# Two layers of a hybrid-attention decoder on one core: where head group C's halves stand, and how its pages are loaded

## The reference, cut to what matters

```python
oa = dilated_attend(qa, ka_all, va_all, wbuf + jnp.arange(t), rel_bias)          # A: 6 heads, window cache
ob = dsa_attend(qb, qi, wi, q_pos, ki_all, gather_kv, ..., rel_bias)             # B: 6 heads, top-k keys, paged
kc_all = jnp.concatenate([paged_rows(cache_c_k), kc], axis=1)                    # C: 4 heads x 64 values, paged
vc_all = jnp.concatenate([paged_rows(cache_c_v), vc], axis=1)
oc = diff_attend(qc, kc_all, vc_all, q_pos, lam_l, lam_init, subln_g_l, rel_bias)
o = jnp.concatenate([oa.reshape(nb, t, -1), ob.reshape(nb, t, -1), oc.reshape(nb, t, -1)], axis=-1)
```

## Time and profile before

| | us |
|---|---|
| median of 3 runs | 1349.34 |
| lowest, highest | 1344.23, 1352.64 |
| the profiled execution | 1351.34 |
| its span | 1349.6 |

### The profile page before, as it was taken

The page is one execution under the profiler, slowest core; times in us unless marked ns, Lnnn a source line. Parts: engine busy times, 40 slices in busy tenths (PEclk is TensorE's granted clock), DMA queues, the critical chain, the costliest instruction groups (busy, mean ns, idle before and its releaser), DMA issues.

```text
span 1349.6 us, 23207 instructions
## 1 busy us (share of the span) xinstructions
PE 1281.5 (95%) x8038; PEld 803.8 (60%) x8038; DVE 495.5 (37%) x1433; ACT 265.4 (20%) x683; POOL 59.9 (4%) x265
## 2 busy tenths in 40 slices
PE   6898899989999999999999999998899999999998
PEld 3544356645657666666666445664556577767775
DVE  1103568865672111011040165876766511101113
ACT  0121144322123111000022112542221411100001
POOL 1000011100001000000010000110100100000000
PEclk9999999998999999999999999998999999999999
DMA  9899899999874687868754688999996456776663
GB/s 376 246 318 280 280 328 360 342 349 350 268 247 151 210 302 251 328 237 322 277 212 158 224 284 285 337 345 351 352 343 224 152 192 210 245 270 217 210 215 138
DMA packets 190814, 363.83 MB, mean 270 GB/s; under 512 B 23072, under 2 KB 141608, under 8 KB 189034
## 3 DMA queue, kind: packets, MB, share of 16 engines
q1 hardware_dynamic: 156192, 345.62, 74.5%
q10 hardware_dynamic: 34506, 16.74, 4.6%
HBM read 354.20 MB, written 58.40 MB: 306 GB/s over the span
## 4 chain that ended last, share of the span: by engine, by line
PE 71%; SPq 15%; DMA 5%; issue 4%; DVE 4%; DVEq 1%; ACT 1%; ACTq 0%
PE psf L1148 23%; PE psf L1623 21%; SPq L556 11%; PE psf L1526 4%; DMA ring<-in_tiles 3%; PE psf L1607 3%; PE psf L1169 2%; PE psf L1350 2%; PE psf L1397 2%; PE psf L1465 2%; PE psf L1232 1%; SPq L566 1%; SPq L548 1%; PE psf L1521 1%; PE psf L1430 1%
## 5 line engine op out<-in xcount | busy, mean ns | idle before, releaser
L1148 PE MATMUL psf<-hT,ring 128*128 128x320 f32 x1184 | 326.3, 435 | 5.5 <-DMA ring<-in_tiles 5.1
L1148 PEld LDWEIGHTS psf<-hT,ring 128*128 128x128 f32 x1184 | 224.1, 191 | 109.7 <-issue 16.7
L1623 PE MATMUL psf<-big,ring 128*128 128x320 f32 x1024 | 278.0, 433 | 2.1 <-DVE big L2113 2.1
L1623 PEld LDWEIGHTS psf<-big,ring 128*128 128x128 f32 x1024 | 193.7, 190 | 86.8 <-issue 3.4
L2113 DVE TENSOR_TENSOR big<-sq 128x320 f32<-128x320 f32 x64 | 31.5, 493 | 239.1 <-ACT sq L1117 238.8
L1723 DVE TENSOR_SCALAR rstd<-psf,adaT 128x256 f32<-128x256 f32 x40 | 19.3, 482 | 235.8 <-PE psf L1623 231.9
L1350 PE MATMUL psf<-big,qs 128*32 128x512 f32 x512 | 69.3, 637 | 9.9 <-DMA big<-in_pool_bk 9.6
L1117 ACT ACTIVATE sq<-psf 128x320 f32<-128x320 f32 x64 | 28.0, 438 | 231.8 <-PE psf L1148 220.9
L1074 ACT ACTIVATE sq<-xT 128x320 f32<-128x320 f32 x32 | 15.1, 471 | 289.9 <-DVE xT L1736 276.7
L1397 PE MATMUL psf<-big,ptbuf 128*32 128x128 f32 x2048 | 64.0, 278 | 4.2 <-DMA big<-in_pool_cv 4.2
L1397 PEld LDWEIGHTS psf<-big,ptbuf 128*32 128x32 f32 x2048 | 55.5, 111 | 10.8 <-issue 9.0
(11 more groups left out here) (219 smaller groups left out, 1351.5 us busy)
## 6 DMA issues: line engine op xcount, KB each, us to landing
ring<-in_tiles SPq DMA_DIRECT2D x246, 512.0 KB, 4.4
big<-in_cache_a SPq DMA_DIRECT2D x64, 768.0 KB, 7.1
out_cache_a<-in_cache_a SPq DMA_DIRECT2D x64, 768.0 KB, 5.4
big<-in_pool_bk SPq DMA_DIRECT2D x128, 192.0 KB, 6.0
big<-in_pool_bv SPq DMA_DIRECT2D x128, 192.0 KB, 6.6
big<-in_pool_cv SPq DMA_DIRECT2D x192, 64.0 KB, 5.3
big<-in_tiles SPq DMA_DIRECT2D x22, 512.0 KB, 7.7
big<-in_pool_ck SPq DMA_DIRECT2D x128, 64.0 KB, 4.1
```

The costliest lines, as they stand in the source:

```text
L1148: ins = pe.matmul(ps[:, 0:T], ring[:, s, k, :], rhs[:, k, :], start=k == 0, stop=k == KD - 1)
L1623: ins = pe.matmul(bank[6 + m % 2][:, 0:T], ring[:, s, k, :], uT[:, KD * q + k, :], start=q + k == 0, stop=q == 3 and k == KD - 1)
```

## The change

Units 0 to 3 now take C's first half of sequences 0 to 3 and units 4 to 7 the second half of the same sequences. Units 8 and up take both halves of sequences 4 to 7 in pairs: 8 and 9 sequence 4, 10 and 11 sequence 5, 12 and 13 sequence 6, 14 and 15 sequence 7. A's and B's sequences are as before. For the last three sequences ACT loads C's pages whole, in rows of 1024 bytes, into one of two stores, for two units at once; SP loads none of C's values for them. Since a unit's half of C no longer goes with A or B, `sbias[0]` and `sbias[1]` now go with C's half; A's rows in them are overwritten by B's (`load_rows`) in each layer and restored before the next. The four `parts` are issued one by one, each one turn ahead of its use.

```diff
-        self.q, self.k, self.qc, self.kc = (QB, KB, QC + 1, KC + 1) if self.second else (QA, KA, QC, KC)
+        self.c, self.half = (n % 4, n // 4) if n < NB else (n // 2, n % 2)
+        self.whole, self.store = n >= NB + 2, n // 2 % 2
+        self.q, self.k, self.v, self.o = (QB, KB, VB, 4) if self.second else (QA, KA, VA, 0)
+        self.qc, self.kc, self.vc, self.oc = QC + self.half, KC + self.half, VC + P * self.half, 3 + 4 * self.half
...
+            def load_rows(e, second):
+
+                for g in range(3):
+                    sp.dma_start(sbias[e][G * g:G * g + 2 * NT, :],
+                                 bass.AP(dist_s.tensor, (HA * second + 2 * g) * row + NT - 1,
+                                         [[row, 2], [H * NDIST - 1, NT], [1, L]])).then_inc(ld_rows[e], 16)
...
-                    if u.n == len(LATE) - 1:
+                    if u.n + 1 in PARTS:
 
                         sp.wait_ge(tile_used, used(MID[l][-1]))
-                        for m in PARTS.values():
-                            sp.dma_start(parts[m].rearrange("p k m -> p (k m)"),
-                                         a["tiles"][l * TILES + WO_AT + m, :, 0:3 * P]).then_inc(ld_parts, 16)
+                        m = PARTS[u.n + 1]
+                        sp.dma_start(parts[m].rearrange("p k m -> p (k m)"),
+                                     a["tiles"][l * TILES + WO_AT + m, :, 0:3 * P]).then_inc(ld_parts[m], 16)
...
+                    if u.n == 4:
+
+                        sp.wait_ge(u_logit.sem, u_logit.done(l, 3))
+                        load_rows(0, True)
+                    if u.n == 7:
+
+                        sp.wait_ge(u_logit.sem, u_logit.done(l, 7))
+                        load_rows(1, True)
...
-                    load_c(l, then, was, 1, range(NPG // 2 if then.second else NPG))
+                    if then.second and not then.whole:
+                        load_c(l, then, pages(then.c, CHECKED), 1, range(NPG // 2))
+                    elif not then.second:
+                        load_c(l, then, was, 1)
...
+                        if l + 1 < DEPTH and d in (10, 12):
+                            load_rows(d // 2 - 5, False)
...
+                def load_whole(pool, places, signal, at):
+
+                    for j in range(NPG):
+                        act.dma_start(places[j // (NPG // 2)][:, j % (NPG // 2), :],
+                                      pool[ds(at[j] + l * N_PHYS, 1)].rearrange("o p w -> (o p) w")).then_inc(signal, 16)
...
+                    then = UNIT[u.n + 3] if u.n in (7, 9, 11) else None
+                    if then:
+
+                        at = pages(then.c, CHECKED)
+                        if u.n == 7:
+                            act.wait_ge(tile_used, used(MID[l][-1]))
+                        act.wait_ge(u_s.sem, u_s.done(l, u.n))
+                        load_whole(a["pool_ck"], whole_k[then.store], ld_wk[then.store], at)
+                    then = UNIT[u.n + 2] if u.n in (8, 10, 12) else None
+                    if then:
...
+                        act.wait_ge(u_o.sem, u_o.done(l, u.n - 1))
+                        load_whole(a["pool_cv"], whole_v[then.store], ld_wv[then.store], at)
...
+                    if u.c != u.b:
+                        zc = TS - NT - NT * u.c
+                        pe.transpose(bank[2][0:TS, 352:384], znew[3 * G:P, zc:zc + TS], ident[3 * G:P, 3 * G:P])
...
+                    if u.n in (NB, NB + 1):
+
+                        dve.wait_ge(ld_rows[u.half], 48 * (2 * l + 1))
...
-                        ins = dve.tensor_copy(oT[q, u.o:u.o + 4, t0:t0 + NT],
-                                              bass.AP(first.tensor, first.offset, [list(first.ap[0]), [2 * NT, 4], [1, NT]]))
+                        part = bass.AP(first.tensor, first.offset, [list(first.ap[0]), [2 * NT, 3], [1, NT]])
+                        dve.tensor_copy(oT[q, u.o:u.o + 3, t0:t0 + NT], part)
+                        ins = dve.tensor_copy(oT[q, u.oc, tc:tc + NT], bank[3][q, P + NT * (6 + half):P + NT * (7 + half)])
```

More of the change, by code:

```diff
@@ L277, in program @@
                  for i, m in enumerate(PARTS.values())}
+        flat = lambda x: x[:, :, :].rearrange("p k t -> p (k t)")
+        four = KD * P
+        whole_k = [[fours(kv[:, s, CK_AT:CK_AT + four]) for s in range(2)],
+                   [fours(flat(hT)[:, 3 * P * len(PARTS):3 * P * len(PARTS) + four]), fours(flat(zT[:, QI:QI + 4, :])[:, 0:four])]]
+        whole_v = [[fours(kv[:, s, CV_AT:CV_AT + four]) for s in range(2)],
+                   [fours(workbuf[:, 0:four]), fours(wkibuf[:, 0:four])]]
         ik = [x[:, 0:PAST].rearrange("p (j w) -> p j w", j=NPG)
@@ L346, in program @@
         ld_more = [sem(f"ld_more{j}") for j in range(2)]
-        ld_parts = sem("ld_parts")
+        ld_parts = {m: sem(f"ld_parts{m}") for m in PARTS.values()}
         ld_late = {i: sem(f"ld_late{i}") for i in HOMED}
@@ L354, in program @@
         ld_dist = sem("ld_dist")
+        ld_wk = [sem(f"ld_wk{s}") for s in range(2)]
+        ld_wv = [sem(f"ld_wv{s}") for s in range(2)]
+        ld_rows = [sem(f"ld_rows{e}") for e in range(2)]
         st_dist = sem("st_dist")
@@ L573, in load_c @@
             def load_c(l, u, at, half, which=range(NPG)):
-                load_pages(l, at, a["pool_cv" if half else "pool_ck"], P * u.second, (ck_in, cv_in)[half][u.s],
+                load_pages(l, at, a["pool_cv" if half else "pool_ck"], P * u.half, (ck_in, cv_in)[half][u.s],
                            (ld_ck, ld_cv)[half][u.s], which)
@@ L670, in load_keys, with pages_of @@
                         load_c(l, u, at, 0)
-                at = pages(2, CHECKED)
+                def pages_of(u):
+                    return pages(u.b if u.second else u.c, CHECKED)
+                at = pages_of(UNIT[2])
                 sp.wait_ge(u_s.sem, u_s.done(l, 0))
@@ L810, in _ @@
                 for u in UNIT:
-                    pool.wait_ge(z_set.sem, z_set.done(l, MADE_AT[QB + 2 if u.second else QC]))
+                    pool.wait_ge(z_set.sem, z_set.done(l, MADE_AT[QB + 2 if u.second else u.qc]))
                     pool.wait_ge(u_s.sem, u_s.free(l, u.n))
-                    t0 = TP + NT * u.b
+                    t0, tc = TP + NT * u.b, TP + NT * u.c
                     for half in range(2):
@@ L1047, in _ @@
                         exp_item(slots[0])
-                    was = at
-                    if NB <= u.n + 3 < UNITS:
-                        at = pages(UNIT[u.n + 3].b, CHECKED)
+                    if u.n + 3 in (NB, NB + 1):
+                        at = pages(UNIT[u.n + 3].c, CHECKED) if u.n + 3 == NB else at
                         load_c_keys(UNIT[u.n + 3], at)
@@ L1906, in read_logits @@
                     dve.wait_ge(u_tp.sem, u_tp.free(l, u.n))
+                    if u.n in (NB, NB + 1):
+                        dve.wait_ge(ld_rows[u.half], 48 * (2 * l + 1))
+                    elif l and u.n in (0, 4):
+                        dve.wait_ge(ld_rows[u.half], 48 * 2 * l)
                     dve.sem_inc(passed, 1)
-                    dve.tensor_tensor_reduce(out=S[:, 0, :], in0=psf[:, 0:L], in1=sbias[u.second][:], scale=1.0,
+                    dve.tensor_tensor_reduce(out=S[:, 0, :], in0=psf[:, 0:L], in1=sbias[u.half][:], scale=1.0,
                                              scalar=-3e38, op0=ALU.add, op1=ALU.max, accum_out=mx[:, u.s, 0:1])
```

57 lines of the change are left out of this document (35 added, 22 removed).

## The result

The changed kernel took **1368.35 us** (median of 4 runs, 1358.74 to 1369.74), the kernel before 1348.24 in runs beside it; the ratio is **1.0145**, 95% interval 1.0118 to 1.0171. The forecast was 1361 us within 1340 to 1372: the range holds it, the side is right (slower), the sum was 8 us too small. By the bound of one per cent it is slower, which had the chance 0.27. The profiled execution took 1367.81 us, its span is 1366.0 against 1349.6.

What follows compares the result with a forecast made beforehand. PE carries 71% of the chain, but in the sample attention data, not arithmetic, decide. Unit 10's wait +4.6 and +3.7 us, unit 11's values +1.4, PE and DVE +2.0: +11.7 on 1349.3 gives 1361 us, range 1340 to 1372.

Steps and rivals of the forecast that it cites:

- two engines: Bias-row DMAs in SP's turns 4 and 7: source's outer dimension 2, so two engines carry 24 rows each, 4.1 us.
- PE and DVE: Units of both layers: one more transpose in 11 units a layer and two more copies per unit, together +2.0 us.
- The price of a set: Three DMAs of 16 bias rows, twice in a layer's units: each set costs 3.7 us of wall where queues overlap.
- The first set ... about 4 us of slack, so no stall there: Bias rows issued in turn 4: unit 6's values, tightest behind them, still land in time, with about 4 us of slack.
- The new wait of DVE: Unit 9's logits, layer 0: DVE must have the second set of bias rows, so it stands 4 to 5 us.
- The later of the two, not their sum: Around units 9 and 10: DVE's wait for bias rows and PE's for unit 10's keys overlap; only the later counts.
- waits for unit 10's `pool_bk` at about 8.5 and 9 us: Sign that the forecast is right: PE's waits for unit 10's B keys grow from 3.91 and 5.49 us to these.
- The packet price: DMA engine time: 11.2 ns fixed per packet plus 38.3 us per MB, so 512 bytes cost 30.8 ns, 1024 bytes 50.4.
- "faster" rival: Bias rows cheap and all six pairs of whole rows a layer pay back, -8.8 us in both layers: 1340 us; chance 0.18.
- Parts: Output-weight parts leave the queue ahead of unit 10's keys: -2.1 us at that wait, +1.05 at unit 11's values, layer 0.
- Theory A: Follow-up runs' theory: the cost is that a 16-row bias DMA with outer source dimension 2 runs on two engines.

## Why the prediction was right and where it was wrong

The range and the side were right, and two engines were the main cause as forecast. But the sum came near by luck in part: a stall that the sum held at nothing cost 8 us, and other terms erred the other way. By place, profiled executions, in us:

| | forecast | measured |
|---|---|---|
| layer 0, first logits to `turn_far` of unit 7 | 0 | +8.0 |
| layer 0, on to unit 10 | +4.6 | +4.4 |
| layer 0, on to the output projection | +1.4 | -2.9 |
| layer 1, up to unit 8 | 0 | +0.5 |
| layer 1, on to unit 10 | +3.7 | +3.4 |
| layer 1, on to the output projection | 0 | +1.3 |
| PE and DVE, wherever | +2.0 | in the rows above |
| dense stretches | 0 | +1.8 |
| sum | +11.7 | +16.4 |

**Two engines: right, and shown.** Widening the DMAs takes 1.05 points out of the change's 1.45, with the same bytes and the same time of issue. Narrow ones cost 1.41% added to the kernel before, wide ones 0.60%. And the packets show bias rows two at a time in the one case and up to eight in the other.

**The price of a set: near, for the first one.** 3.7 us were forecast; 0.97 MB are missing behind it in layer 0, 2.8 us, and its own bytes (0.2 MB, 0.6 us) come on top. Part of that is SP's issue, in which the engines ran dry. In layer 1 only 0.28 MB are missing in the 20 us around the first set. The two engines were held longer than the 4.1 us of the forecast: 48 rows took 9.4 to 11.3 us of engine time in all, so 4.7 to 5.6 on each of two, spread over 5.3 to 8.3.

**"The first set ... about 4 us of slack, so no stall there": wrong, in layer 0.** This is the step that failed. PE waited 4.95 us and lost another 1.7 by the lower clock. The slack was spent twice. I had priced SP's issue of three DMAs at 1.3 us and called it covered by data under way; it took 2.12 us, and the cover ran out while it lasted, since the engines emptied meanwhile (7 and 3 tenths ahead of the dip). Unit 6's values were issued 3.3 us later; the slowest landed 8.1 us after its issue, not 5.6; and PE wanted them at 253.75, 1.6 us earlier than before, as its first logits had begun 2.0 us earlier. Against that the slack of the page that lands last was not 4 us but 2.3 (247.4 + 5.6 = 253.0, wanted at 255.32; I had reckoned with a page of median landing): 3.3 + 2.5 + 1.6 - 2.3 = 5.1 us, against 4.95 measured. In layer 1 the wait for unit 6's values is 0.84 us, where the kernel before had 1.53, so the step held there. With 8-row DMAs SP issues as long; layer 0 then has no wait for these values, layer 1 one of 3.06 us.

**The new wait of DVE: right in kind, its size in neither layer.** Forecast 4 to 5 us; measured 3.02 and 8.14. In layer 0 the stall at unit 6 had moved PE and with it DVE's need of the rows.

**"The later of the two, not their sum": right in layer 1, in part in layer 0.** In layer 1 PE's old wait for unit 10's keys, 5.49 us, became 0.19, and 6.62 us stand before it on DVE's account. In layer 0 the 2.15 us on DVE's account are followed by 2.60 for C's whole keys, which ACT issues last. So "waits for unit 10's `pool_bk` at about 8.5 and 9 us", which I had named as the mark, was wrong: the same loss has another name and place in the profile, and its sum by place (+4.4 and +3.4 us) came out as forecast.

**The packet price: right.** The changed kernel's DMA from 308 to 345 us:

```profile
DMA packets 10971, 13.58 MB, mean 367 GB/s; under 512 B 1220, under 2 KB 10965, under 8 KB 10965
...
q1 hardware_dynamic: 7718, 10.54, 82.0%
q10 hardware_dynamic: 3247, 2.95, 24.2%
q8 instruction: 4, 0.07, 0.8%
```

107.0% of 16 x 37 us are 633 us; 10971 x 11.2 ns and 13.58 x 38.3 us give 643. (A share above 1.0 needs no second queue: q1 alone stood at 104.8%.) But it bought nothing. The forecast counted +2.2 - 0.7 for whole rows at units 10 to 12 in layer 0 and +1.1 in layer 1; measured without the exchange they cost 0.5%, some 7 us, and from unit 12 on alone as much, where I had counted nothing. Why is open. The "faster" rival (packets decide) falls.

**Parts: right in the mechanism, nothing in the sum.** At unit 10's wait in layer 0 -2.1 us were forecast, -2.7 measured with the parts alone, and 4.1 us of new waits followed (1.40 and 2.68), where I had expected 1.05.

**PE and DVE, +2.0: too much.** With all of it in and neither exchange nor whole rows the ratio is 0.9982. The new transposes and the split copies of the outputs are short, as priced (duration ns, min/median/max), and `turn_near` waits for the copies 1.9 us in three places, before 2.3 in two:

```profile
L1446 PEld LDWEIGHTS psf<-ident,znew x22: 103/105/125, 226.7 to 1018.9; 32*64 32x64 f32 x22
...
L2044 DVE COPY oT<-psf x44: 166/180/186, 247.6 to 1041.5; 64x24 f32<-64x24 f32 x44
...
L2045 DVE COPY oT<-psf x44: 146/155/163, 247.7 to 1041.6; 64x8 f32<-64x8 f32 x44
```

**What stays open.** Theory A accounts for 15 of the 20 us between the medians (1368.35 - 1353.08). The rest, about 5 us, is some of whole rows and some of the exchange's bytes, and doesn't add up: exchange (8 rows a DMA) alone +0.6%, whole rows alone +0.5%, both +0.4%, and the exchange with halves +0.9%. The first of these had the four parts ahead of the second set and the others had not, so their differences are not those of the named edits alone; no run adds the exchange to the parts alone. Single executions of the changed kernel lie up to 11 us apart (1358.74 to 1369.74), so the waits of one profiled execution can't settle a few tenths of a per cent.

## What to carry to other kernels

Count the engines of a DMA before its bytes: four sets of 0.2 MB cost 1.4% in three DMAs each, and 0.6% in six each. A wait that goes at one unit in a stretch where data decide is a wait at the next: three edits here (the second set earlier, whole keys earlier, the parts) moved one by 2 us or more and left the time as it was. Slack ahead of an inserted transfer is used up by its issue on the queue's engine first, and then by its landing.

## What the runs showed of the hardware

Of DMAs whose source is [2][8] rows of 4128 bytes, to 16 partitions, two rows are under way at a time, and 48 rows took 5.3 to 9.1 us in the three kernels that have them. In DMAs of [8] rows five to nine are under way at the most, and 48 rows took 2.1 to 5.7 us in the six kernels that have them. The Trainium skill ("DMA: Bandwidth & Descriptors", on why a DMA increments its semaphore by 16) gives the rule of the divisor of the outer dimension; the trace agrees.

SP itself can be held in an issue. Some 20 us after the first set one of eight issues of a 64 KB page took 3.7 us where the others took 0.38 (line L569 from 256.8 us, ns, min/median/max), and in layer 1 one took 2.3:

```profile
L569 SPq DMA_DIRECT2D big<-in_pool_cv x8: 375/381/3707, 256.9 to 260.2; - x8
```

In the kernel before the longest of the same eight was 0.59 us. I had no term for that. With the second set a turn earlier, still narrow, one at the same place took 3.2 us; with the narrow exchange on the kernel before the longest there was 1.8. That narrow DMAs are the cause is not shown.

A three-dimensional issue of bias rows took SP 0.58 to 0.79 us, a two-dimensional one of half the rows mostly 0.28 to 0.37.

With two queues and B's pages in both mixes, C in rows of 1024 bytes went at 366 to 368 GB/s, C in rows of 512 at 343 to 353. The Trainium skill ("DMA: Bandwidth & Descriptors", specifications) states that 512 bytes reach line rate; these runs show 4 to 7% less in the mix.
